# Five products instead of six per k tile in 158 projection units of a hybrid attention and SSD decoder step

## What is computed

```
h = rmsnorm(x, g_pre) * (1 + scale) + shift            # scale, shift, gate = silu(c) @ w_ada + b_ada
q, k, v, z_a, z_b, xbc, dt_raw, r_a, r_b = split(h @ w_in)   # D_MODEL 2048
A = (dilated attention of q, k, v in 3 groups of 8 heads x 128, merged by log-sum-exp) * silu(z_a)
B = rmsnorm_groups(SSD(silu(conv4(xbc)), dt) * silu(z_b)) * g_ssm
merged = sigmoid(r_a) * (A @ w_o_a) + sigmoid(r_b) * (B @ w_o_b)
y = x + gate * rmsnorm(merged @ w_o, g_post)
```

## Time and profile before

| | |
|---|---|
| device time, 3 runs | 3028.29, 3034.97 (median), 3036.03 us |
| the profiled execution | 3028.3 us, span 3026.5 us, granted PE clock 0.997 on the mean |
| busy: PE, PEld, DVE, ACT, POOL | 98%, 94%, 62%, 29%, 40% of the span |
| L1374, L1375, L1376 | 5744 matmuls each |
| DMA | 704.86 MB, mean 233 GB/s |

### The profile page before, as it was taken

How to read it: one execution, slowest core, us unless ns; L and a number is a source line. 1 busy time by engine, 2 the same in 40 slices (tenths; PEclk the granted TensorE clock), 3 DMA queues, 4 the chain that set the end, 5 groups by cost and what they waited for, 6 DMA issues and landing times.

```text
span 3026.5 us, 52526 instructions
## 1 busy us (share of the span) xinstructions
PE 2973.9 (98%) x22660; PEld 2835.5 (94%) x22660; DVE 1867.1 (62%) x2044; ACT 867.3 (29%) x1239; POOL 1213.2 (40%) x576
## 2 busy tenths in 40 slices
PE   6999999999999999999999999999999999999998
PEld 4898999999999999999999999999999989999886
DVE  3303688888785787878887756766668665211302
ACT  3111222333233223233222242333323343211312
POOL 1133444433333333334444544444444434444332
PEclk9999999999999999999999999999999999999999
DMA  8878786554446786647567666656556666876643
GB/s 335 327 272 320 313 302 242 211 204 128 148 141 212 268 286 236 205 172 259 228 249 251 244 229 214 235 197 238 209 201 236 228 204 213 291 255 250 251 174 139
DMA packets 220460, 704.86 MB, mean 233 GB/s; under 512 B 26739, under 2 KB 129899, under 8 KB 170795
## 3 DMA queue, kind: packets, MB, share of 16 engines
q1 hardware_dynamic: 157686, 471.33, 44.7%
q0 software_dynamic: 5248, 174.60, 14.2%
q10 hardware_dynamic: 57296, 55.59, 5.5%
HBM read 630.85 MB, written 245.17 MB: 289 GB/s over the span
## 4 chain that ended last, share of the span: by engine, by line
PE 95%; DMA 2%; DVE 1%; SPq 0%; issue 0%; ACT 0%; POOL 0%; DVEq 0%; POOLq 0%; ACTq 0%
PE acc L1374 25%; PE acc L1376 25%; PE acc L1375 25%; PE ps_s L1247 2%; PE ps_s L1528 1%; PE ps_s L1413 1%; PE ps_w L1433 1%; PE ps_s L1494 1%; PE ps_t L1388 1%; PE ps_s L1421 1%; PE ps_s L1613 1%; PE ps_s L1612 1%; PE ps_s L1614 1%; DMA w_raw<-in_w_ada_t 1%; PE ps_s L1515 0%; PE ps_s L1414 0%
## 5 line engine op out<-in xcount | busy, mean ns | idle before, releaser
L893 POOL TENSOR_TENSOR w_lo<-w_raw,w_hi 128x1024 fp32r<-128x1024 f32 (+1 forms) x416 | 1074.5, 2601 | 1765.7 <-ACT w_hi L944 1765.7
L1374 PE MATMUL acc<-act,w_hi 128*128 128x288 f32 x5744 | 1718.3, 299 | 1.8 <-POOL w_lo L893 1.8
L1376 PE MATMUL acc<-act,w_lo 128*128 128x288 f32 x5744 | 1691.9, 295 | 0.0
L1375 PE MATMUL acc<-act,w_hi 128*128 128x288 f32 x5744 | 1691.8, 295 | 0.0
L1374 PEld LDWEIGHTS acc<-act,w_hi 128*128 128x128 f32 x5744 | 1078.2, 188 | 26.1 <-issue 21.9
L1375 PEld LDWEIGHTS acc<-act,w_hi 128*128 128x128 f32 x5744 | 1078.6, 188 | 1.1
L1376 PEld LDWEIGHTS acc<-act,w_lo 128*128 128x128 f32 x5744 | 1077.7, 188 | 0.0
L944 ACT ACTIVATE w_hi<-w_raw 128x1024 fp32r<-128x1024 f32 (+1 forms) x418 | 403.8, 1015 | 475.3 <-PE acc L1376 192.6
L1814 DVE TENSOR_TENSOR side<-side 128x2048 f32<-128x2048 f32 x96 | 282.3, 2941 | 98.0 <-DMA side<-in_vals_t 85.3
L1012 ACT ACTIVATE ev<-acc 128x576 f32<-128x576 f32 x144 | 93.7, 651 | 823.7 <-PE acc L1376 820.3
L1785 DVE TENSOR_TENSOR side<-side 128x2048 f32<-128x2048 f32 x96 | 269.1, 2803 | 84.7 <-DMA side<-in_keys_t 82.0
(11 more groups left out here) (331 smaller groups left out, 2741.0 us busy)
## 6 DMA issues: line engine op xcount, KB each, us to landing
w_raw<-in_w_in_t SPq DMA_DIRECT2D x160, 1024.0 KB, 7.5
out_s_kv<-in_cache_a_w POOLq DMA_DIRECT2D x80, 1632.0 KB, 9.0
side<-in_keys_t SPq DMA_DIRECT2D x52, 1024.0 KB, 8.1
side<-in_vals_t SPq DMA_DIRECT2D x52, 1024.0 KB, 8.0
w_raw<-in_w_ada_t SPq DMA_DIRECT2D x40, 1024.0 KB, 7.7
out_s_kv<-in_cache_a_w POOLq DMA_DIRECT2D x24, 1344.0 KB, 7.9
w_raw<-in_w_o_b_t SPq DMA_DIRECT2D x16, 1024.0 KB, 7.2
w_raw<-in_w_o_t SPq DMA_DIRECT2D x16, 1024.0 KB, 8.6
```

Of the source, the lines that this page charges most:

```text
L893: nc.gpsimd.tensor_tensor(dst, raw[:, SLOT[s], ks, 0:cols], wh[:, u % 2, ks, 0:cols].bitcast(F32), ALU.subtract).then_inc(lo, 1)
L1374: nc.tensor.matmul(out, wh[:, c, k, 0:cols], high, start=(k == 0), stop=False)
L1375: nc.tensor.matmul(out, wh[:, c, k, 0:cols], low, start=False, stop=False)
L1376: mm = nc.tensor.matmul(out, wl[:, c, k, 0:cols], high, start=False, stop=(k == kt - 1))
```

## The change

Of the q, k, v, r, s, x and z units, all but units 0 and 1 are PAIRED (158 units). Their tokens are cut 256 + 320 instead of 288 + 288. `front` takes the place of the first half: one matmul of 512 columns with `wh` over both limbs of 256 tokens, low limb into columns 0 to 255 of bank 0, high limb into columns 256 to 511, then one matmul of 256 columns with `wl` on the high limb, into the latter. `back` does the other 320 tokens with three matmuls in bank 1. ACT first copies the 256 low sums to SBUF (`store_low`), DVE adds them to the high sums in PSUM (`fold_low`), then ACT reads the 576 sums, which lie side by side over both banks (`store_sums`), and counts `evac`.

```diff
+FRONT = 256
+PAIRED = [kind in "qkvrsxz" and u >= 2 for u, kind in enumerate(KINDS)]
+FOLDS = [sum(PAIRED[:u + 1]) for u in range(NU)]
...
+        def limbs(k):
+            return act[:, k:2 * KT:KT, 0:FRONT]
+        def sums(u):
+            n = FRONT if PAIRED[u] else HALF
+            return acc[u % 2][0:unit_cols(u)[1], :, :].rearrange("p a n -> p (a n)")[:, 512 - n:512 - n + TOK]
+        def low_sums(u):
+            return acc[u % 2][:, 0, 0:FRONT]
+        def high_sums(u):
+            return acc[u % 2][:, 0, FRONT:2 * FRONT]
+        def front_home(u):
+            return (zs[:, UNITS[u][2], :] if KINDS[u] == "s" else ev[:, u % 2, :])[:, 0:FRONT]
...
+            def store_low(u):
+                act_e.wait_ge(used, u + 1)
...
+                nc.scalar.activation(front_home(u), low_sums(u), ACT.Copy).then_inc(low_out, 1)
+            def store_sums(u):
...
+                act_e.wait_ge(folded, FOLDS[u])
...
+                nc.scalar.activation(out, sums(u), func).then_inc(evac, 1)
...
-                if KINDS[u] not in "ABO":
+                if PAIRED[u]:
+                    store_low(u)
+                elif KINDS[u] not in "ABO":
                     store_unit(u)
...
                 if u + 2 < NU and u + 1 not in (A0, O0):
                     high(u + 2)
+                if PAIRED[u]:
+                    store_sums(u)
...
+            def front(u, k):
+                c, both = u % 2, acc[u % 2][:, 0, :].rearrange("p (a n) -> p a n", a=2)
+                nc.tensor.matmul(both, wh[:, c, k, :], limbs(k)[:, ::-1, :], start=(k == 0), stop=False)
+                mm = nc.tensor.matmul(high_sums(u), wl[:, c, k, :], hH[:, k, 0:FRONT], start=False, stop=(k == KT - 1))
+                return mm
+            def back(u, k):
+                c, out = u % 2, acc[u % 2][:, 1, 0:TOK - FRONT]
+                nc.tensor.matmul(out, wh[:, c, k, :], hH[:, k, FRONT:TOK], start=(k == 0), stop=False)
+                nc.tensor.matmul(out, wh[:, c, k, :], hL[:, k, FRONT:TOK], start=False, stop=False)
+                return nc.tensor.matmul(out, wl[:, c, k, :], hH[:, k, FRONT:TOK], start=False, stop=(k == KT - 1))
...
+                if PAIRED[u]:
+                    for k in range(kt):
+                        if half == 0 and 2 * k == kt:
+                            pe.wait_ge(lo, 2 * u + 2)
+                        mm = (back if half else front)(u, k)
+                    if half == 1:
+                        mm.then_inc(used, 1)
+                    return
...
+            def fold_low(u):
+                dve.wait_ge(low_out, FOLDS[u])
+                TT(high_sums(u), high_sums(u), front_home(u), ALU.add).then_inc(folded, 1)
...
             for half in range(2 * NU):
                 u = half // 2
                 if half % 2 == 0 and u:
+                    if PAIRED[u - 1]:
+                        fold_low(u - 1)
```

More of the change, by code:

```diff
@@ L441, in phase_all @@
         gate_d, gate_out = sems("gate_d", "gate_out")
-        hi, lo, used, evac = sems("hi_done", "lo_done", "mm_done", "evac_done")
+        hi, lo, used, low_out, folded, evac = sems("hi_done", "lo_done", "mm_done", "low_out", "fold_done", "evac_done")
         stored = sems("stored0", "stored1")
@@ L989, in ev_free @@
                     act_e.wait_ge(o_t, n + 1)
+            def store_low(u):
+                act_e.wait_ge(used, u + 1)
+                if KINDS[u] == "s":
+                    after(act_e, yz, 6 * UNITS[u][1])
+                    if UNITS[u][1] == 0:
+                        act_e.wait_ge(oa_out, 16 * H)
+                        act_e.wait_ge(dt_c, 4)
+                else:
+                    ev_free(u)
+                nc.scalar.activation(front_home(u), low_sums(u), ACT.Copy).then_inc(low_out, 1)
+            def store_sums(u):
+                c, (col, cols) = u % 2, unit_cols(u)
+                kind, g, n = UNITS[u]
+                act_e.wait_ge(folded, FOLDS[u])
+                func = {"s": ACT.Silu, "z": ACT.Silu, "r": ACT.Sigmoid}.get(kind, ACT.Copy)
+                out = zs[:, n, :] if kind == "s" else ev[:, c, :]
+                nc.scalar.activation(out, sums(u), func).then_inc(evac, 1)
+                if STORED[u]:
+                    act_e.wait_ge(evac, EVACS[u])
+                    t = SEQ if kind in "qk" else TOK
+                    act_e.dma_start(S["projT"][col:col + cols, 0:t], ev[:, c, 0:t]).then_inc(stored[c], 16)
             def store_unit(u):
```

## The result

After the change the kernel takes 3143.93 us (median of 4 runs, 3134.41 to 3153.71), against 3033.70 us for the kernel before on the same chip (4 runs, 3028.29 to 3036.03): ratio 1.0366, 95% interval 1.0326 to 1.0406, 110 us slower. My 3102 had the sign and most of the mechanism, but the time lies 6 us above the end of my range (3138). The profiled execution took 3137.96 us, its span is 3136.2.

The account below looks back on a forecast made before the run. PE was taken to bound the kernel. The profiled 3028.3 us, less 33.7 saved, plus 94 of stalls and 7 of clock, gave 3095.6; the median was forecast at 3102 us, range 3048 to 3138.

Parts of the forecast that it names:

- What bounds the kernel: PE holds 95% of the chain; nobody waits for DVE's grains, so their lateness is free before the change.
- The saving, 33.7 us: On PE, one product fewer per k tile saves a fixed 13.3 ns: 0.213 us a unit, 158 units.
- One break in the moving operand, 0 to 9.4 us: The 512 column product's operand is two blocks; up to 3.7 ns a break, taken as 0.
- a short product held up by its weight load, 0 to 33.7 us: The 256 column product might be slowed by its weight load, 0 to 13.3 ns each; taken as 0.
- The shape of a unit: First part shrinks from 6.40 to 5.55 us, so in k and v units PE reaches the transposes 0.85 us earlier.
- The new chain: `evac` needs low copy (0.38), DVE's addition (0.41) and ACT's pass (0.65); after DVE's previous half it takes 1.27 us.
- The stalls, 94 us: PE waits for `evac`: units 11 to 19 30 us, 25 to 35 24, 58 to 76 25, 80 to 110 15.
- The clock, 7 us: Half clock on PE after nine stalls over 3.3 us outside the gate units, 1.5 us each, half taken off the next stall.
- The sum: Profiled 3028.3 - 33.7 + 94 + 7 = 3095.6; median forecast 3102 us, 67 us or 2.2% slower.
- DVE catches up for good: Rival: DVE keeps a lead won once, only the first stall of each stretch remains, 19 us; 3020 us, chance 0.14.
- milder stalls: Rival: chunks land sooner and grains collide less with POOL, so stalls cost 47 us; 3052 us, chance 0.16.
- The change doesn't save what it says: Rival: weight loads pace the 256 column product, or the fixed part is below 13.3 ns; 3136 us, chance 0.08.

Follow-up runs that it names:

- e10: Kernel before with key and value chunks issued two halves earlier in SyncE's order; 3032.73 us.
- e6: Changed kernel with key and value chunks issued two halves earlier in SyncE's order; 3054.27 us.
- e1: Changed kernel with its five products but without ACT's low copy, DVE's addition and the wait for it; 3026.54 us.
- e5: e2 with ACT's copy of 256 columns, and DVE's addition of them in place of the bare signal; 3148.43 us.
- e4: Changed kernel with the fold earlier in DVE's program, ahead of grains and softmax step, in units 11 to 21, 25 to 35, 58 to 76 and some others; 3034.72 us.
- e2: Kernel before, six products; ACT empties the bank after high(u+2) and a bare DVE signal at the fold's place, no copy or addition; 3092.55 us.
- e12: e2 with a DVE pass over 8 columns of the bank in place of the bare signal; 3144.18 us.
- e3: Changed kernel with 13 or 20 identity products on PE just ahead of its wait in nine units; 3144.71 us.

## Why the prediction was right in sign and too low in size

- **What bounds the kernel** (PE, and nobody waits for the grains): right. e10 shows that the lateness of keys is free in before, e6 that it is not in after.
- **The saving, 33.7 us:** the step that failed first. The 147 ns of the 320 columns came true, and the 347 of the pair in the fast units, but by luck: the 512 column product takes 4 ns more than the 227 of my sum and the 256 column one 4 less than its 120. The fixed 13.3 ns came from one half of one unit of before; the other half runs at 131.6 ns. And in half of the units or more the front pair takes 354 ns and not 347. That leaves 12 us by the paces of e1 and 10 by those of after, of which 4 arrive in e1 and 6 are left as the remainder in after. The 2.5 ns that the Trainium skill gives for the fixed part (TensorE: Matmul & The Clock Gate, section "Wait — 56ns, not 53.3ns?") would make 6.3 us by the estimate in the prediction. With the mean of both halves, 132.5 ns, the line to the earlier trace rows (94.2 ns for 224 columns) leaves 11.4 ns, so the figure for one product stays at odds with these rows, though the total it leads to came nearer than mine.
- **One break in the moving operand, 0 to 9.4 us; a short product held up by its weight load, 0 to 33.7 us; both taken as 0:** the slow pair, 7 ns longer, comes to 8 us in e1 and 10 in after, at the edge of the first bound. About 6 of the 7 ns fall on the 512 column product, which has the break, and even in fast units it is 4 ns above. So my 3.7 ns a break was too little, if it is the break; it came from durations of transposes (328 against 272), and a duration isn't what a product costs. The 256 column product is faster than forecast in both states (116 and 117 ns), so nothing shows a weight load that holds it up beyond the 120. Which pace a unit has is the same within it, differs between executions for some units, and not for others; no run takes it apart.
- **The shape of a unit** (0.85 us sooner in k and v units): right as a length (5.55 us, or 5.66 with the slow pair), though against 6.32 and not 6.40 before; e5 gives no sign that it added to the stalls at the token transposes. What I missed is that every other product behind the shorter part comes sooner too. e1 shows it: 4.1 us more of idle time in units 110 to 160, where I had taken 0, at most 10, for x and s units.
- **The new chain:** fold, copy and pass at their forecast prices. `store_samples` behind `store_sums` was missing, 0.3 us.
- **The stalls, 94 us:** PE is idle 80 us more. The mechanism was right; the sum is nearer than its parts, as units 11 to 19 fell short (21 us of 30), units 86 to 109 too (7 of 15), and the x and s units, put at 0, have 7. Unit 25 has 4.8 (forecast 5.1), unit 58 has 6.4 (6.7), unit 74 has 6.2 (6.5), unit 105 has 6.2 (8). That a stall lets VectorE catch up was right (units 26, 28 and 30 have none), the amounts less so: I had 1.0 and 3.3 us for units 28 and 30, and 3.8 for unit 29, which has 6.4. Its place, VectorE's half 2u - 1 with the grain, is confirmed by e4, and that the grain must be *over* by e2 against e12.
- **The clock, 7 us:** the second step that failed. I had the earlier trace rows, one wait of 4.2 us with 3.4 us at half clock, and so counted stalls over 3.3 us outside the gate units, once each; no row showed such a bound. In after the wait of 2.1 us in unit 13 is followed by 3.4 us of work at 0.50, and the wait of 3.1 us in unit 63 by 5.5. And the 6.4 us wait that ends at 576.52 in unit 29 is followed by 5.8 us of work at a granted clock of 0.50:

```profile
572.30:576.50 4.20, 0.00 (x0) 0.01 (x1) 4.17 (x4) 0.80 (x2) 0.00 (x0) 0.51 1.05 416
576.60:582.40 5.80, 5.80 (x23) 5.80 (x24) 4.87 (x3) 0.60 (x1) 0.00 (x0) 0.50 0.74 266
```

and the gate units, with waits of 0.7 to 4.2 us one upon the other, had 31.9 us of work at that clock, where I had counted none beyond before's. The sum by rows is 36 us against 7. In e3 it could not be won back piece by piece, so the firm comparison is that of idle time and slow products together, 116 us against my 101.
- **The sum:** relative to before I forecast 67 us, and 110 were measured. Of the 43 between them 28 are the saving (33.7 less 6), 29 the clock (36 less 7), and -14 the stalls (80 less 94). As the 6 is a remainder, the account closes by construction; only the 36 and the 80 were read.
- **The rivals.** "DVE catches up for good" was refuted, and so was "milder stalls" (47 us; PE is idle 80 us more); e4 and e6 show what it would have taken. "The change doesn't save what it says", 3136, came nearest to the time, for its reason and one more; I gave it 0.08. The range ended at its value, which added no clock beyond mine: the bound of the clock's cost was missing from the range.

## What to carry to other kernels

Before an engine with long work in its program gets a short step on the path of another, find what stands ahead of that step at its place, and put it there ahead of the long piece: here the same step of 0.43 us made the kernel 110 us slower behind the grains, and ahead of them 4 us slower, which the interval (0.9998 to 1.0018) doesn't tell from no change. Look then for a way from the late step back to its own cause (a load that is issued behind another one's release): if there is one, a stall does not pay for the next, and then an earlier load is a cure too: 90 of the 110 us in e6, where moving the step gave 109. And take a product's pace from both halves of the code before, at several places, when the gain is a difference of two of them.

## What was not expected of the hardware

- A signal that VectorE's program gives by itself, not attached to an operation, was seen by ScalarE 0.07 us after the start of the 2.29 us reduction ahead of it (e2, unit 14; 41 of 53 such signals were given within 0.04 us of the start of the operation ahead). So such a signal doesn't say that the work ahead of it is done. One attached to a pass of 8 columns at the same place cost 52 us more over the kernel (e12 against e2).
- The same two products, 512 and 256 columns with their weight loads, run at 347 or at 354 ns a pair (231 + 116 or 237 + 117), at one pace for a whole unit, in after 354 in all units from 2 to 10 and from 97 to 109 that could be read. The 288 column products of before run at 131.6 ns in the first half and 133.3 in the second half of unit 54. Why is open.
- The half clock begins inside a long wait: in unit 29 at the latest 4.2 us ahead of its end (the first of the two windows above), which leaves it another 5.8 us of PE's work.
